# Key norms into the input projection, low-rank activations into the mLSTM, S5 rounds and bonus rows into the RWKV chunks

## The reference

```python
z = jnp.matmul(h, w_in).astype(f32)          # one projection for mLSTM and RWKV
...                                          # mLSTM in chunks on the first columns
zs = zr + (prev - zr) * mu                   # token shift of the RWKV columns
r, kr, vr = zs[..., :HALF], zs[..., HALF:2*HALF], zs[..., 2*HALF:3*HALF]
w_log = -softplus(-(w0 + tanh(zs[..., o1:o2]) @ w_up)) - 0.5
decay = exp(-exp(w_log))
a = sigmoid(a0 + zs[..., o2:o3] @ a_up)
g = sigmoid(zs[..., o3:]) @ g_up
kk = (kr * k_k).reshape(b, T, 8, 64)
kk = kk * rsqrt(maximum(sum(kk * kk, -1), 1e-24))
kr = kr * (1.0 + (a - 1.0) * k_a)
yr, S = rwkv7_recurrence(r, decay, kr, vr, kk, a, S0)
yr = head_layer_norm(yr) + sum(r * kr * r_k, -1) * vr     # the bonus
y = concatenate([y_m, yr * g], -1) @ w_out
```

## Time and profile before

| | |
|---|---|
| median of 3 runs | 1789.22 us (1788.43 to 1800.36) |
| the profiled execution | 1786.72 us, span on the chip 1784.9 us |
| PE, PEld | 1620.8 us (91%), 1565.6 us (88%) |
| DVE, ACT, POOL | 1063.9 us (60%), 475.0 us (27%), 878.3 us (49%) |
| granted TensorE clock | 0.946 of full, mean over the span |
| DMA | 149.09 MB, mean 84 GB/s |

### The profile page before, as it was taken

One profiled execution on the slowest core, in us unless ns is written; L12 is line 12 of the kernel. 1 busy time (PEld: TensorE's weight loads), 2 busy tenths in 40 slices (PEclk: granted clock), 3 DMA queues, 4 the chain that ended last, 5 costly groups with the idle time before them and its releaser, 6 DMA issues. The chain is left out here.

```text
span 1784.9 us, 35376 instructions
## 1 busy us (share of the span) xinstructions
PE 1620.8 (91%) x14910; PEld 1565.6 (88%) x14910; DVE 1063.9 (60%) x1539; ACT 475.0 (27%) x689; POOL 878.3 (49%) x731
## 2 busy tenths in 40 slices
PE   6999985539996999999989998999899999998996
PEld 5999984338995999999989998977799999998996
DVE  4816767785655767776651327687576777664012
ACT  4002124441114243333320013131424333332001
POOL 4667688940100744444456655710274444445663
PEclk8999987669998999999989999998999999999998
DMA  4222111125100222222212221254422222221222
GB/s 174 83 71 82 59 73 54 48 74 163 68 3 27 87 87 82 82 82 82 82 55 87 77 86 59 82 193 121 119 88 85 83 82 82 83 82 56 84 86 83
DMA packets 50680, 149.09 MB, mean 84 GB/s; under 512 B 17553, under 2 KB 19233, under 8 KB 48417
## 3 DMA queue, kind: packets, MB, share of 16 engines
q1 hardware_dynamic: 50592, 147.91, 26.1%
HBM read 127.58 MB, written 19.13 MB: 82 GB/s over the span
## 5 line engine op out<-in xcount | busy, mean ns | idle before, releaser
L279 PE MATMUL PP<-arena_r,dual_r 128*128 128x288 f32 (+1 forms) x6428 | 1117.7, 298 | 48.2 <-DVE arena_r L266 16.0
L279 PEld LDWEIGHTS PP<-arena_r,dual_r 128*128 128x128 f32 (+1 forms) x6428 | 966.8, 190 | 52.0 <-issue 25.9
L279 PE MATMUL PP<-hT_r,dual_r 128*128 128x288 f32 (+1 forms) x2176 | 646.8, 297 | 0.0
L266 POOL TENSOR_TENSOR dual_r<-w_ring,dual_r 128x1024 fp32r<-128x1024 f32 (+1 forms) x198 | 484.5, 2447 | 18.1 <-ACT dual_r L1901 5.0
L266 POOL TENSOR_TENSOR dual_r<-w_ring,cst 128x1024 fp32r<-128x1024 f32 (+1 forms) x114 | 215.1, 1887 | 501.3 <-PE PP L279 353.1
L279 PEld LDWEIGHTS PP<-hT_r,dual_r 128*128 128x128 f32 (+1 forms) x2176 | 410.1, 188 | 1.4
L269 DVE SCALAR_TENSOR_TENSOR rowbuf<-rowbuf,convp 128x592 f32<-128x592 f32 x176 | 271.3, 1542 | 91.5 <-ACT rowbuf L1924 90.9
L279 PE MATMUL PP<-arena 64*64 64x64 f32 (+6 forms) x3640 | 192.8, 246 | 23.5 <-ACT arena L2037 7.4
L279 PEld LDWEIGHTS PP<-arena 64*64 64x64 f32 (+2 forms) x3640 | 172.6, 141 | 41.5 <-issue 13.3
L266 DVE TENSOR_TENSOR xT<-PP,xT 128x576 f32<-128x576 f32 x32 | 24.2, 758 | 262.4 <-PE PP L279 262.4
L1901 ACT ACTIVATE dual_r<-w_ring 128x1024 fp32r<-128x1024 f32 x84 | 89.2, 1062 | 332.2 <-PE PP L279 332.2
(11 more groups left out here) (268 smaller groups left out, 1347.9 us busy)
## 6 DMA issues: line engine op xcount, KB each, us to landing
w_ring<-in_w SPq DMA_DIRECT2D x150, 512.0 KB, 3.6
w_ring<-in_w_down SPq DMA_DIRECT2D x32, 448.0 KB, 3.3
w_ring<-in_w_down SPq DMA_DIRECT2D x16, 512.0 KB, 3.5
xT<-in_x SPq DMA_DIRECT2D x8, 576.0 KB, 7.5
gy_scratch<-dual SPq DMA_DIRECT2D x1, 2304.0 KB, 13.1
dual<-gy_scratch SPq DMA_DIRECT2D x1, 2304.0 KB, 13.9
out_y<-hT SPq DMA_DIRECT2D x4, 576.0 KB
xT<-in_C SPq DMA_DIRECT2D x1, 2064.0 KB, 9.4
```

The lines of the kernel that those rows point to most:

```text
L266: return eng.tensor_tensor(out, a, b, op)
L279: return nc.tensor.matmul(out, lhsT, rhs, start=start, stop=stop)
```

## The change

Five moves, none of which alters what is computed.

1. *Key norms.* The squares are now made on ACT straight from `zr`, with `k_k` as the scale, behind the tap of `k = 9`, into rows of the gates' buffer that are then free. The sums over heads (`kk_norms`) are eight matmuls on PE, at a second break in the projection's loop, ahead of the tiles of `k = 12` and 13. DVE limits the 8 rows before it takes out the last tile, ACT takes the root behind its last tap, DVE inverts behind the first chunk's keys in the mLSTM. The prologue keeps the spreading by `headrow` and one product per pair, which takes in `k_k`.
2. *Low-rank activations.* Tanh and sigmoid on ACT move into the mLSTM, behind chunk 1.
3. *Rounds.* The affine step becomes an Identity on ACT behind the two sigmoids, written to `rkp`. The gate matmuls and their copies move behind the first pair's low-rank product; they use `PP[2]` and `PP[3]` in turn.
4. *Bonus.* The bonus product moves from the rounds to DVE at the start of chunks 4 to 7, from the decayed rows, whose decays cancel.
5. *S5 rounds.* The two kernel rounds move into the chunk after the samples, using bank 7, the eight rounds of transposes into the last chunk and its tail, using bank 4 alone. The store of `FZT` moves on SP behind the sample states; POOL and DVE wait for it before the first ConvFFN uses that buffer.

The diff, cut to its core:

```diff
-    sp.wait_ge(S("s5_evac"), 10)
-    sp.dma_start(fzt_scr, FZT).then_inc(S("s5_out"), 16)
...
     sp.wait_ge(S("rs_st"), 1)
     sp.dma_start(o["sS"], SS).then_inc(S("sS_written"), 16)
+    sp.wait_ge(S("s5_evac"), 10)
+    sp.dma_start(fzt_scr, FZT).then_inc(S("s5_out"), 16)
     sp.wait_ge(S("rk_st"), NCR + 1)
...
+    def kk_norms():
+        for p in range(RP):
+            pe.wait_ge(S("rw_kksq"), p + 1)
+            for a in range(2):
+                last = mm(PP[3][64:72, a, 0:TH], col8(p), kksq[p][:, a * TH:(a + 1) * TH], p == 0,
+                          p == RP - 1)
+        last.then_inc(S("rw_kkn"), 1)
...
     def rwkv():
+        pe.wait_ge(S("rw_kkrow"), 2)
         pe.wait_ge(S("ycat"), NCH + 1)
+        pe.wait_ge(S("ml_sst"), 8)
...
-    pe.wait_ge(S("rw_lora"), 2)
-    pe.wait_ge(S("ml_sst"), 8)
-    for p in (1, 2, 3, 0):
-        if p == 0:
-            pe.wait_ge(S("rw_kkrow"), 1)
-        for a in range(2):
-            last = mm(PP[p][:, a, 0:TH], lora[:, 1, p * P:(p + 1) * P], zr[:, 13, a * TH:(a + 1) * TH])
-        last.then_inc(S("rw_gate"), 1)
-    pe.wait_ge(S("rw_kkrow"), 2)
-    for p in range(RP):
-        pe.wait_ge(S("rw_gatec"), 4)
         for a in range(2):
             last = mm(PP[p][:, a, 0:TH], headrow[:, p, :], kkrow[:, a * TH:(a + 1) * TH])
         last.then_inc(S("rw_kkn"), 1)
...
+    def lora_up(p):
         for q, r in ((0, 0), (1, 64)):
             for a in range(2):
                 last = mm(PP[2 * (p % 2) + q][:, a, 0:TH], lora[r:r + 64, 0, p * P:(p + 1) * P],
                           zr[r:r + 64, 12, a * TH:(a + 1) * TH])
         last.then_inc(S("rw_up"), 1)
+
+    pe.wait_ge(S("rw_lora"), 2)
+    pe.wait_ge(S("rw_kkrow"), 4)
+    lora_up(0)
+    pe.wait_ge(S("rw_kkrow"), 6)
+    for q, p in enumerate((1, 2, 3, 0)):
+        if q >= 2:
+            pe.wait_ge(S("rw_gatec"), q - 1)
+        for a in range(2):
+            last = mm(PP[2 + q % 2][:, a, 0:TH], lora[:, 1, p * P:(p + 1) * P],
+                      zr[:, 13, a * TH:(a + 1) * TH])
+        last.then_inc(S("rw_gate"), 1)
+    pe.wait_ge(S("rw_gatec"), 4)
+    lora_up(1)
+    for p in (2, 3):
+        pe.wait_ge(S("rw_sig"), 2 * (p - 1))
+        lora_up(p)
     pe.wait_ge(S("rw_sig"), 8)
...
+    def s5_kernel(i):
+        pe.wait_ge(S("s5_made"), 3)
+        pe.wait_ge(S("rk_st"), NST[AT_S + 1] + 1)
+        if i:
+            pe.wait_ge(S("s5_evac"), i)
+        for e in range(16):
+            q, j = e % 4, e // 4
+            g = 16 * i + e
+            last = mm(bank(7)[32 * q:32 * q + 32, P * j:P * j + P],
+                      FZ[:, g, BL - 2:BL, :].rearrange("p s c -> p (s c)"),
+                      Gy[:, g, 0:BL, :].rearrange("p s c -> p (s c)"))
+        last.then_inc(S("s5_sq"), 1)
+
+    def s5_transpose(i):
+        pe.wait_ge(S("rk_tokc"), 2 * NCR + 2)
+        pe.wait_ge(S("s5_evac"), i)
+        for e in range(4):
+            g = 4 * (i - 2) + e
+            last = nc.tensor.transpose(bank(4)[:, P * e:P * e + P],
+                                       FZ[:, g, :, :].rearrange("p s c -> p (s c)"), ident)
         last.then_inc(S("s5_sq"), 1)
...
-    pe.wait_ge(S("s5_evac"), 10)
...
     if i:
         seq_r1(i - 1)
+    if i == AT_S + 1:
+        s5_kernel(0)
+    if not after:
+        s5_transpose(2)
     level(i, 1)
     if i:
         seq_u(i - 1)
+    if not after:
+        s5_transpose(3)
     level(i, 2)
     if i:
         seq_ys(i - 1)
     if TOP[i] == 5:
         for k in (3, 4, 5):
             level(i, k)
+            if i == AT_S + 1 and k == 5:
+                s5_kernel(1)
+            if not after:
+                s5_transpose(k + 1)
             if i == AT_S + 1:
...
     seq_r1(NCR)
+    s5_transpose(7)
     bonus(0)
     bonus(1)
+    s5_transpose(8)
     seq_u(NCR)
     bonus(2)
+    s5_transpose(9)
     bonus(3)
     seq_ys(NCR)

+    pe.wait_ge(S("s5_evac"), 10)
...
-    project("e_in", None, 11, mlstm_columns)
+    project("e_in", None, {11: mlstm_columns, 14: kk_norms})
...
+        if k == 9:
+            act.wait_ge(S("shifted"), 8)
+            act.wait_ge(S("ml_rows"), 2)
+            act.wait_ge(S("ml_bcast"), 1)
+            for p in range(RP):
+                A(kksq[p], zr[:, 4 + p, :], ACT.Square, scale=v_("k_k", p)).then_inc(S("rw_kksq"), 1)
+    act.wait_ge(S("rw_kkrow"), 1)
+    A(kkrow, kkrow, ACT.Sqrt).then_inc(S("rw_kksqrt"), 1)
...
         ml_square(c)
+        if c == 1:
+            act.wait_ge(S("shifted"), 14)
+            A(zr[0:64, 12, :], zr[0:64, 12, :], ACT.Tanh).then_inc(S("rw_lora"), 1)
+            A(zr[:, 13, :], zr[:, 13, :], ACT.Sigmoid).then_inc(S("rw_lora"), 1)
         if c == NCH - 1:
             ml_scale(0, NCH)
     ml_scale(NCH, NCH + 1)

-    act.wait_ge(S("shifted"), 14)
-    A(zr[0:64, 12, :], zr[0:64, 12, :], ACT.Tanh).then_inc(S("rw_lora"), 1)
-    A(zr[:, 13, :], zr[:, 13, :], ACT.Sigmoid).then_inc(S("rw_lora"), 1)
-    for p in range(RP):
-        act.wait_ge(S("rw_kk"), p + 1)
-        A(AR[:, p, 1, :], AR[:, p, 0, :], ACT.Square).then_inc(S("rw_kksq"), 1)
-    act.wait_ge(S("rw_kkrow"), 1)
-    A(kkrow, kkrow, ACT.Sqrt).then_inc(S("rw_kksqrt"), 1)
-    act.wait_ge(S("ml_supd"), 8)
-    for q, p in enumerate((1, 2, 3, 0)):
-        act.wait_ge(S("rw_gate"), q + 1)
-        A(halves(hT[:, 4 + p, :]), pair(p), ACT.Copy).then_inc(S("rw_gatec"), 1)
     for p in range(RP):
...
     for q, b in ((0, "w0"), (1, "a0")):
-        A(halves(prep[:, q, p % 2, :]), pair(2 * (p % 2) + q), ACT.Sigmoid,
-          bias=v_(b, p)).then_inc(S("rw_sig"), 1)
+        last = A(halves(prep[:, q, p % 2, :]), pair(2 * (p % 2) + q), ACT.Sigmoid, bias=v_(b, p))
+        if q == 0:
+            last.then_inc(S("rw_sig"), 1)
+        else:
+            chain(last)
+    A(rkp[:, p, :], prep[:, 1, p % 2, :], ACT.Identity, bias=omka[:, p:p + 1],
+      scale=v_("k_a", p)).then_inc(S("rw_sig"), 1)
+    if p == 0:
+        act.wait_ge(S("ml_supd"), 8)
+        for q, g in enumerate((1, 2, 3, 0)):
+            act.wait_ge(S("rw_gate"), q + 1)
+            A(halves(hT[:, 4 + g, :]), pair(2 + q % 2), ACT.Copy).then_inc(S("rw_gatec"), 1)
...
     for i in range(NCR + 1):
         if i:
             r1_copy(i - 1)
+            if i == AT_S + 1:
+                s5_copy(0)
+            if i == NCR:
+                s5_copy(2)
             u_copy(i - 1)
+            if i == NCR:
+                s5_copy(3)
             y_copy(i - 1)
+            if i == AT_S + 1:
+                s5_copy(1)
         if i < NCR:
             tok_copy(i + 1)
+    for k in (4, 5, 6):
+        s5_copy(k)
     r1_copy(NCR)
+    s5_copy(7)
...
+    if k == 13:
+        V.tensor_scalar(omka, vec[:, VEC["k_a"]:VEC["k_a"] + 4], -1.0, 1.0, ALU.mult, ALU.add)
+        dve.wait_ge(S("rw_kkn"), 1)
+        V.tensor_scalar(halves(kkrow), PP[3][64:72, :, 0:TH], 1e-24, None, ALU.max).then_inc(
+            S("rw_kkrow"), 1)
...
     keys(0)
+    dve.wait_ge(S("rw_kksqrt"), 1)
+    V.reciprocal(kkrow, kkrow).then_inc(S("rw_kkrow"), 1)
...
     def rwkv_prep():
-        chain(V.tensor_scalar(omka, vec[:, VEC["k_a"]:VEC["k_a"] + 4], -1.0, 1.0, ALU.mult, ALU.add))
         dve.wait_ge(S("ycat"), NCH + 1)
         for p in range(RP):
-            V.tensor_scalar(AR[:, p, 0, :], zr[:, 4 + p, :], v_("k_k", p), None,
-                            ALU.mult).then_inc(S("rw_kk"), 1)
-        dve.wait_ge(S("rw_kkn"), 1)
-        V.tensor_scalar(halves(kkrow), PP[0][64:72, :, 0:TH], 1e-24, None, ALU.max).then_inc(
-            S("rw_kkrow"), 1)
-        dve.wait_ge(S("rw_kksqrt"), 1)
-        V.reciprocal(kkrow, kkrow).then_inc(S("rw_kkrow"), 1)
-        for p in range(RP):
             dve.wait_ge(S("rw_kkn"), p + 2)
-            tt(V, halves(AR[:, p, 0, :]), halves(AR[:, p, 0, :]), pair(p), ALU.mult).then_inc(
-                S("rw_kkrow"), 1)
+            stt(halves(AR[:, p, 0, :]), halves(zr[:, 4 + p, :]), v_("k_k", p), pair(p), ALU.mult,
+                ALU.mult).then_inc(S("rw_kkrow"), 1)
         dve.wait_ge(S("rw_kkrow"), 6)
         for p in range(RP):
             ld, a, cum, ex, em = (prep[:, k, p % 2, :] for k in range(5))
             dve.wait_ge(S("rw_sig"), 2 * p + 2)
-
             chain(V.tensor_tensor_scan(cum, c_("scan64", T), ld, 0.0, ALU.mult, ALU.add))
             tt(V, ex, cum, ld, ALU.subtract).then_inc(S("rw_cum"), 1)
-            kk, r, kr = AR[:, p, 0, :], zr[:, p, :], zr[:, 4 + p, :]
+            kk, kr, ka = AR[:, p, 0, :], zr[:, 4 + p, :], rkp[:, p, :]
             chain(tt(V, BK[:, p, 0, :], kk, a, ALU.mult))
-            chain(V.tensor_scalar(a, a, v_("k_a", p), omka[:, p:p + 1], ALU.mult, ALU.add))
-            chain(tt(V, a, a, kr, ALU.mult))
-            chain(stt(rkp[:, p, :], r, v_("r_k", p), a, ALU.mult, ALU.mult))
+            chain(tt(V, ka, ka, kr, ALU.mult))
             dve.wait_ge(S("rw_exp"), p + 1)
             tt(V, BK[:, p, 0, :], BK[:, p, 0, :], em, ALU.mult)
-            tt(V, BK[:, p, 1, :], a, em, ALU.mult)
```

(47 more changed lines are left out.)

17 lines of the change are left out of this document (5 added, 12 removed).

## The result

The changed kernel takes 1798.9 us (median of 20 runs, 1793.18 to 1803.92) against 1790.99 us for the kernel before, measured beside it; the ratio is 1.0048, with a 95% interval of 1.0036 to 1.0059. The forecast was 1788 with a range of 1778 to 1797, so the time lies outside it, on the slow side. It is within 1% of the kernel before, and with 0.04 on either side the forecast had left 0.92 for that.

A forecast was written before the change was run, and what follows sets the result against it. Bounds: PE in the projection, a DVE-ACT-PE chain in the mLSTM, DVE in the rounds, PE with DVE in the chunks. Terms -4.6 - 0.8 + 4.55 = -0.85 against 1789.22 gave 1788.4, rounded 1788; range 1778 to 1797.

The forecast's parts named there:

- norms in the projection: Projection's end: eight norm matmuls stop a saturated PE, 0.50 each, +4.0; squares on ACT hide.
- mLSTM (activations, DVE meeting POOL): mLSTM: uncovered tanh, sigmoid and two table loads +3.9, DVE meeting POOL's long operations elsewhere +2.6.
- last update to first scan: Prologue before the rounds: products, norms and root leave the path; 12.4 remains, so the first scan starts at 339.6.
- four rounds: Prologue's four rounds, one per pair of heads: 13.2 each beside POOL, 7.3 alone, ending at 386.2 against 390.81.
- end of rounds to first level: Between rounds and first level: 6.9 instead of 7.7 without S5 there, half clock lasting part of it, -0.8.
- S5 kernel rounds, chunks 0 to 1: Chunks: each kernel round costs 0.9 at full clock; the first counts +0.9, the second hides in PE's wait.
- last chunk and tail: Last chunk and tail: the S5 transposes, four at 0.55, delay levels and bonus matmuls, +3.65.
- the sentence on SP: SP's queue: transfers start in chunk 2, over 80 us before the output projection, so weights come in time; cost 0.
- POOL's S5 work: Prologue: POOL's S5 work waits for none of the moved norm work and still ends near 377.
- the +2.4: Prologue's head-row matmuls: allowance for half clock, half of the extra over 5.56 that 8 x 1.0 would take.
- that rival: mLSTM: each of two table switches costs its 1.28 once more, the mLSTM ends 2.6 later, total 1790; chance 0.04.
- The rival on the slow side: Last chunk and tail: eight transposes sharing one PSUM bank wait for ACT's copies, 9.2 instead of 3.65; 1794, chance 0.20.

The follow-up runs named there:

- e5: The change with x loaded behind the mLSTM states' store, and the image's and sample states' stores and first output weights behind the last chunk; 1800.41 us, ratio 1.0055.
- e6: The kernel of e5 plus 4.7 MB copied from device memory to device memory, issued after the state of prompt chunk 2; 1803.7 us in one execution.
- e3: The change with tanh and sigmoid of the low-rank columns back on ACT behind the mLSTM's last scaling; 1799.56 us, ratio to before 1.0030.
- e11: The changed kernel a third time, unchanged, for one more profile; 1798.0 us.

## Why the prediction was wrong, step by step

Three profiles of the change and two of before, taken from the projection's first break on, give each step (means) without the luck of that break. The sum stands beside the 7.9 of the medians. (The prediction's working carries 327.1 on as 327.2, a slip of 0.1.)

| step | forecast | measured |
|---|---|---|
| norms in the projection | +4.0 | +4.2 |
| mLSTM (activations, DVE meeting POOL) | +6.5 | +7.4 |
| last update to first scan | -11.1 | -10.8 |
| four rounds | -4.1 | -2.8 |
| end of rounds to first level | -0.8 | -0.2 |
| S5 kernel rounds, chunks 0 to 1 | +0.9 | +1.9 |
| chunk 2, meeting POOL's weight splits | 0 | -1.1 |
| burst, and POOL's splits, in chunks 4 and 5 | 0 | +4.9 |
| last chunk and tail | +3.65 | +3.5 |
| sum | -0.9 | +7.0 |

**The step that failed** is the sentence on SP: the transfers start later, "so its weights still come in time". That was true (29.6 from the head norm to the first tile, 29.8 before), and the wrong question. I asked who waits for the transfers, and not what runs while they move, and put the move at nothing. Before, the burst meets 186 matmuls in 10 us; in chunk 4 it meets 404, which take 15 us undisturbed and 22 here. e5 takes the burst out and the loss in the chunks goes; e6 puts another in and the loss is back. Of the 8 between forecast and measurement 3.8 is this step: the 4.9 of chunks 4 and 5 less the 1.1 that POOL's splits no longer cost in chunk 2.

**The second failed step** is that POOL's S5 work "doesn't wait for any of this, so it still ends near 377". It ended at 383.25:

```profile
381.59 1.66 POOL L267 TENSOR_TENSOR dual<-dual 128x512 f32<-128x512 f32 x1
```

POOL splits the projection's weights as PE uses them, so what stops PE there should delay POOL's S5 as well. The profiles bear it out: in the ten profiles without the edit of e3 it ends 145.6 to 146.3 after the copy of the last tile begins, whatever else was changed (in the four with that edit it is 148.4 to 150.9). So all three of the first rounds ran beside POOL, and the rounds gained 2.8 and not 4.1.

**The S5 kernel rounds** were priced at full clock, 0.9 for the one on the path. The first ran at half clock and took 1.93, and chunk 1 is 2.35 longer than before in two profiles of the change, with a mean granted clock of 0.88. In e11 the clock there is 0.94, as before, and the chunk is 0.93 longer: the price held at the clock that it was meant for. The second round, 1.08, was hidden, as forecast: it fills a wait of 0.88 for DVE, and from the matmuls ahead of it to those behind it takes 3.51 for 3.45.

**What held.** The norms' matmuls cost 4.05 for 4.0. The square root and the reciprocal hid (from the last tile's copy to the next decay 13.83 against 13.88). Tanh and sigmoid cost their 3.9 (the next outputs waited 4.87 for 0.95). The table loads cost their load and nothing more, so that rival is out. The product over 4128 columns stayed at 4.44 beside POOL, while POOL's own operation beside it took 5.76 instead of 1.05: a wait for a whole operation. The Trainium skill (SBUF — State Buffer, Who interferes with whom) says that the port pair that the two share is an exclusive lock. This row agrees with it. The first rounds took 13.8 and 13.4 for 14.2 and 13.2, and the head-row matmuls ran at half clock throughout, 8.01, which is what the +2.4 had allowed for.

**The rival on the slow side**, the single bank that serialises the transposes, gave 1794 with the right sign and the wrong mechanism: the tail is 3.5 longer, as the forecast had it, and PE has 4.4 more work in it with a single wait of 0.17 for a copy. By this trace PE was short of time there, not of a bank; no run gave the transposes more banks there.
